# Writing the engine loops over pairs of experts out as straight code with constant waits, in a two-layer decoder with eight routed experts

## The reference, cut to what matters

```
logits = (t @ w_router).astype(jnp.float32)
top_v, top_i = lax.top_k(logits, TOP_K)                 # TOP_K = 2
top_w = jax.nn.softmax(top_v, axis=-1)
combine = jnp.sum(jax.nn.one_hot(top_i, N_EXPERTS) * top_w[..., None], axis=1)
out = jnp.zeros_like(t)
for e in range(N_EXPERTS):                              # N_EXPERTS = 8
    out = out + combine[:, e:e+1] * swiglu(t, w1[e], w3[e], w2[e])
# swiglu(x, w1, w3, w2) = (silu(x @ w1) * (x @ w3)) @ w2
# w1, w3: 1024 x 2816, w2: 2816 x 1024, float32
```

## Time and profile before

| what | value |
|---|---|
| median of 3 executions | 1356.41 us (1354.2 to 1357.6) |
| the profiled execution | 1354.73 us, of which the span of its instructions 1350.5 us |
| instructions in the profile | 17653 |
| PE busy | 1312.4 us, 97% |
| DVE busy | 1061.7 us, 79% |
| ACT busy | 877.3 us, 65% |
| POOL busy | 65.6 us, 5% |
| HBM read | 376.12 MB, 282 GB/s over the span |

### The profile page before, as it was taken

How to read it: one execution, slowest core, us unless ns; L and a number is a source line. 1 busy time by engine, 2 the same in 40 slices (tenths; PEclk the granted TensorE clock), 3 DMA queues, 4 the chain that set the end, 5 groups by cost and what they waited for, 6 DMA issues and landing times.

```text
span 1350.5 us, 17653 instructions
## 1 busy us (share of the span) xinstructions
PE 1312.4 (97%) x6066; PEld 1076.6 (80%) x6066; DVE 1061.7 (79%) x983; ACT 877.3 (65%) x870; POOL 65.6 (5%) x45
## 2 busy tenths in 40 slices
PE   7899999999999999799999999999999999999998
PEld 6688888888888788678888778788888788788776
DVE  5857756665457667699898799898898897998996
ACT  6567444444365664577777677777777777777774
POOL 0500000000006010000000000000000000000200
PEclk9999999999999999899999999999999999999999
DMA  9654546555555544289998899998999997999993
GB/s 360 242 190 133 167 146 221 184 187 187 192 183 175 168 150 163 94 302 369 388 384 324 316 410 372 377 374 293 389 405 380 368 357 281 411 386 385 410 355 141
DMA packets 105488, 382.12 MB, mean 283 GB/s; under 512 B 11952, under 2 KB 11952, under 8 KB 105392
## 3 DMA queue, kind: packets, MB, share of 16 engines
q1 hardware_dynamic: 103632, 375.11, 76.2%
q0 software_dynamic: 1616, 5.77, 1.1%
q10 hardware_dynamic: 144, 0.01, 0.0%
HBM read 376.12 MB, written 4.72 MB: 282 GB/s over the span
## 4 chain that ended last, share of the span: by engine, by line
PE 83%; DVE 6%; DMA 5%; ACT 2%; issue 2%; POOL 1%; SPq 1%; POOLq 0%; DVEq 0%; ACTq 0%
PE ps L391 26%; PE ps L393 25%; PE ps L392 25%; DMA raw<-in_units 4%; DVE wl L386 3%; PE ps L881 3%; ACT wh L378 1%; PE ps L1175 1%; DMA cols<-y_rows,yidx 1%; DMA y_rows<-xs 1%; POOL rst L514 1%; PE ps L933 0%; SPq L371 0%; DVE turn_t L1350 0%; POOL back L562 0%
## 5 line engine op out<-in xcount | busy, mean ns | idle before, releaser
L386 DVE TENSOR_TENSOR wl<-raw,wh 128x2048 fp32r<-128x2048 f32 x351 | 802.3, 2295 | 179.2 <-ACT wh L378 170.8
L378 ACT ACTIVATE wh<-raw 128x2048 fp32r<-128x2048 f32 x351 | 673.7, 1920 | 227.0 <-PE ps L393 206.3
L391 PE MATMUL ps<-wh,XT_h 128*128 128x512 f32 x1228 | 491.3, 400 | 15.4 <-DVE wl L386 12.7
L393 PE MATMUL ps<-wh,XT_l 128*128 128x512 f32 x1228 | 480.4, 391 | 0.0
L392 PE MATMUL ps<-wl,XT_h 128*128 128x512 f32 x1228 | 479.3, 390 | 0.0
L391 PEld LDWEIGHTS ps<-wh,XT_h 128*128 128x128 f32 x1228 | 231.1, 188 | 68.0 <-DVE wl L386 12.5
L393 PEld LDWEIGHTS ps<-wh,XT_l 128*128 128x128 f32 x1228 | 231.0, 188 | 50.3
L392 PEld LDWEIGHTS ps<-wl,XT_h 128*128 128x128 f32 x1228 | 231.5, 189 | 44.9
L391 PE MATMUL ps<-wh,moe_gT_h 128*128 128x512 f32 x352 | 138.0, 392 | 0.0
L393 PE MATMUL ps<-wh,moe_gT_l 128*128 128x512 f32 x352 | 137.1, 390 | 0.0
L392 PE MATMUL ps<-wl,moe_gT_h 128*128 128x512 f32 x352 | 137.0, 389 | 0.0
(11 more groups left out here) (235 smaller groups left out, 909.9 us busy)
## 6 DMA issues: line engine op xcount, KB each, us to landing
raw<-in_units SPq DMA_DIRECT2D x704, 512.0 KB, 5.9
y_rows<-xs POOLq DMA_DIRECT2D x7, 512.0 KB, 7.4
mix<-in_xT SPq DMA_DIRECT2D x2, 512.0 KB, 5.6
raw<-in_units SPq DMA_DIRECT2D x4, 256.0 KB, 8.4
h<-in_x SPq DMA_DIRECT2D x1, 1024.0 KB, 12.1
out<-h SPq DMA_DIRECT2D x2, 512.0 KB, 3.0
rows<-in_rows SPq DMA_DIRECT2D x1, 896.0 KB, 15.1
cols<-in_cols SPq DMA_DIRECT2D x1, 512.0 KB, 14.5
```

What stands on the lines that cost most here:

```text
L378: nc.scalar.activation(wh[:, U.split_slot(j), :], raw[:, U.raw_slot(j), :], ACT.Copy).then_inc(hi_ready, 1)
L386: nc.vector.tensor_tensor(wl[:, s, :], raw[:, U.raw_slot(j), :], wh[:, s, :].bitcast(F32), ALU.subtract).then_inc(lo_ready, 1)
L391: nc.tensor.matmul(o, xh, bh, start=start, stop=False)
L393: return nc.tensor.matmul(o, xl, bh, start=False, stop=stop)
```

## The change

The loops over pairs of SP, POOL, ACT, PE and DVE are written out: Python loops over the experts issue the same calls with integers in place of the loop's register. All waits get constants, and SP's DRAM addresses become constants. The calls for each expert, their order, the places and the data are those of before. The loop over overflows is not touched.

```
--- before.py
+++ after.py
@@ -478,12 +478,9 @@
                     U = Units(DENSE_BASE)
                     for u in range(FFN_UNITS):
                         load_unit(sp, U, u, DENSE_BASE + u)
-            with sp.Fori(0, E // 2) as i:
-                U = Units(MOE_BASE, i, 2 * FFN_UNITS)
-                for half in range(2):
-                    for u in range(FFN_UNITS):
-                        j = half * FFN_UNITS + u
-                        load_unit(sp, U, j, 2 * FFN_UNITS * i + (MOE_BASE + j))
+            U = Units(MOE_BASE)
+            for j in range(E * FFN_UNITS):
+                load_unit(sp, U, j, MOE_BASE + j)
 
             sp.wait_ge(table_ready, 1)
             n_over = sp.value_load(otab[0:1, 0:1], min_val=0, max_val=3)
@@ -551,10 +548,8 @@
                 rows_of = y_d[0:Y_ZERO, :].rearrange("(e r) d -> e r d", r=P)[p]
                 pool.dma_start(rows_of, xs3[:, b, :]).then_inc(y_sent, 16)
 
-            store_rows(0, 0)
-            with pool.Fori(0, E // 2 - 1) as i:
-                store_rows(2 * i + 1, 1)
-                store_rows(2 * i + 2, 0)
+            for p in range(E - 1):
+                store_rows(p, p % 2)
             pool.wait_ge(yidx_ready, 1)
             pool.wait_ge(y_sent, 16 * E)
             for t in range(TT):
@@ -860,12 +855,10 @@
 
             gather_copy(0, 0)
             gather_copy(0, 1)
-            expert(0, 0, Units(MOE_BASE), 0, FFN_UNITS + 1, None)
-            with act.Fori(0, E // 2 - 1) as i:
-                U = Units(MOE_BASE + FFN_UNITS, i, 2 * FFN_UNITS)
-                expert(2 * i + 1, 1, U, 0, FFN_UNITS + 1, 8 * i + 8)
-                expert(2 * i + 2, 0, U, FFN_UNITS, FFN_UNITS + 1, None)
-            expert(E - 1, 1, Units(MOE_BASE), (E - 1) * FFN_UNITS, FFN_UNITS - 1, None, None, 0)
+            U = Units(MOE_BASE)
+            for p in range(E - 1):
+                expert(p, p % 2, U, p * FFN_UNITS, FFN_UNITS + 1, 4 * p + 4 if p % 2 else None)
+            expert(E - 1, 1, U, (E - 1) * FFN_UNITS, FFN_UNITS - 1, None, None, 0)
             act.wait_ge(table_ready, 1)
             n_over = act.value_load(otab[0:1, 0:1], min_val=0, max_val=3)
             with act.If(n_over > 0):
@@ -1241,12 +1234,10 @@
             for t in range(TT):
                 last = nc.tensor.matmul(ps[:, 3, 0:E], ones[:, :], routed[:, t, :], start=t == 0, stop=t == TT - 1)
             last.then_inc(counted, 1)
-            expert(0, 0, Units(MOE_BASE), 0, None, 8, None)
-            with pe.Fori(0, E // 2 - 1) as i:
-                U = Units(MOE_BASE + FFN_UNITS, i, 2 * FFN_UNITS)
-                expert(2 * i + 1, 1, U, 0, None, 8 * i + 8, (2 * i + 4, 8 * i + 8))
-                expert(2 * i + 2, 0, U, FFN_UNITS, None, 8 * i + 16, None)
-            expert(E - 1, 1, Units(MOE_BASE), (E - 1) * FFN_UNITS, None, 4 * E, None, 0)
+            U = Units(MOE_BASE)
+            for p in range(E - 1):
+                expert(p, p % 2, U, p * FFN_UNITS, None, 8 * ((p + 2) // 2), (p + 3, 4 * p + 4) if p % 2 else None)
+            expert(E - 1, 1, U, (E - 1) * FFN_UNITS, None, 4 * E, None, 0)
             pe.wait_ge(table_ready, 1)
             n_over = pe.value_load(otab[0:1, 0:1], min_val=0, max_val=3)
             with pe.If(n_over > 0):
@@ -1762,12 +1753,9 @@
                     for r in range(4):
                         add_back(scatter_at, e, r)
 
-            expert(0, 0, Units(MOE_BASE), 0, 0, rank, FFN_UNITS + 1, None)
-            with dve.Fori(0, E // 2 - 1) as i:
-                U = Units(MOE_BASE + FFN_UNITS, i, 2 * FFN_UNITS)
-                expert(2 * i + 1, 1, U, 0, 2 * i + 1, rank, FFN_UNITS + 1, 2 * i + 2)
-                expert(2 * i + 2, 0, U, FFN_UNITS, 2 * i + 2, rank, FFN_UNITS + 1, None)
             U = Units(MOE_BASE)
+            for p in range(E - 1):
+                expert(p, p % 2, U, p * FFN_UNITS, p, rank, FFN_UNITS + 1, p + 1 if p % 2 else None)
             expert(E - 1, 1, U, (E - 1) * FFN_UNITS, E - 1, rank, FFN_UNITS - 1, None, 0)
             dve.wait_ge(table_ready, 1)
             n_over = dve.value_load(otab[0:1, 0:1], min_val=0, max_val=3)
```

## The result

| | before | changed |
|---|---|---|
| median of 5 executions | 1354.2 us (1351.49 to 1357.6) | 1343.73 us (1342.63 to 1346.29) |
| profiled execution | 1354.73 us | 1346.29 us |
| its span | 1350.5 us | 1344.2 us |
| outside the span | 4.23 us | 2.09 us |

The ratio is 0.9926, interval 0.9902 to 0.9949: 10 us less, where 7.6 were forecast (1356.41 - 1348.8, from the median of three on record).

The account below looks back on a forecast made before the run. PE, busy 97% of the span, was taken as the bound; 3.54 us from PE's branches and 3.56 from SP's, off 1356.41, gave 1349.3, taken as 1348.8 us. The 8-in-10 range was 1345.5 to 1353.5.

Parts of the forecast that it names:

- The reading of the bound: Whole kernel: PE is busy for 97% of the span, so only what makes PE stand still can be won.
- step 1: Where experts 3 and 5 begin: PE's two branches back go, giving 1.45 + 2.09 = 3.54 us.
- Step 2: At the start of experts 2, 4 and 6: SP's three branches back go, giving 3.56 us.
- only the branches of PE count: Rival, experts 2 and 6: late units come from DMA traffic after each gather, SP's silence only coincides; 1352.9 us, chance 0.18.
- Step 3: Engines' waits: constants in place of computed ones change nothing, cost 0, as register instructions are hidden or fall into idle time.
- its span and what lies around it: Whole execution of 1354.73 us: taken as span 1350.5 us and 4.23 us around it.
- step 4: Added code: nothing runs that did not run, instruction reads stay the same, and the final part just comes earlier.
- The base: Whole kernel: the starting time was 1356.41 us, the median of the runs shown, 1.7 us above the profiled execution.
- The guess that the spread would shrink: Between runs: part of the spread may be SP's silences of varying length, which would go.
- memory sets the pace: Rival, even experts: once PE stops pausing, weights come late and the time is given back; 1356 us, chance 0.10.
- straight code is read too late: Rival, PE's written-out code: sequential reads miss, about 1.77 us at each of 23 blocks; about 1390 us, chance 0.06.

Follow-up runs that it names:

- before_pad: Kernel before plus 205 never-executed instructions in PE's overflow loop, moving PE's last code to 179 in its block: 1355.07 us against 1355.04, ratio 0.999.
- pe_only: Kernel before with only PE's loop written out: 1347.06 us, ratio 0.9949.
- sp_pe: Kernel before with the loops of SP and PE written out, those of ACT, DVE and POOL kept: 1345.18 us, ratio 0.993.
- rest_only: Kernel before with only the loops of ACT, DVE and POOL written out: 1355.6 us against 1354.3, ratio 1.0002.
- after_pad: Changed kernel plus 51 never-executed instructions in PE's overflow loop, moving PE's last code to 230 in its block: 1346.57 us, ratio 0.9934.
- after2: Changed kernel, unchanged, run again for a second profile: 1344.56 us.
- before: The kernel before the change, with its loops: median 1354.2 us, profiled execution 1354.73 us.
- both: Changed kernel with DVE's last-expert row additions moved behind its last split and PE's last wait moved into the untaken overflow branch: 1339.12 us, ratio 0.9874.
- after_pad2: Changed kernel with the same 51 never-executed instructions, run again beside the unpadded changed kernel on one chip: 1347.37 us.
- after: First profile of the changed kernel: profiled execution 1346.29 us, median 1343.73 us, ratio 0.9926.
- before2: Kernel before, unchanged, run again for a second profile: 1354.47 us.
- pause: Changed kernel with added PE waits, without a branch, where experts 1, 3, 5 and 7 begin: 1356.41 us, ratio to the kernel before 1.0019.

## Why the prediction was wrong, point by point

- **The reading of the bound and step 1's mechanism: right, its size too small.** Both gaps were the branch, and nothing took their place. 3.54 us is what that one profile held; other profiles of looped PE code show 4.0 to 5.2 us, and up to 1.7 us (2.8 in before_pad) of slow clock behind a gap. No row of the profile read had a clock under 1.00 in the experts, so the prediction had no such term. By the median spans, `pe_only` gained 1350.2 - 1344.65 = 5.55 us, 2 more than forecast.
- **Step 2: right in kind, too large in size.** With PE straight, SP's silences cost 1.7 us in the profile and 1.9 in the median, not 3.56; in the profile read they had cost more in expert 2. That the sum fits (7.10 forecast for the experts, 7.30 between the two profiles, 5.55 + 1.85 = 7.4 by the median spans) is luck: one term was too small by about as much as the other was too large. The rival "only the branches of PE count" is refuted by sp_pe against pe_only. It counted expert 4, which lost nothing at its start, against the silence; that silence was the shortest of the three (5.53 us, against 7.71 and 6.39). SP's rounds end 18.3 us before PE gets there (762.53 - 744.20), not 17; no term uses it.
- **Step 3: right.** No cost is seen in rest_only, and the even experts of sp_pe stand at the floor of 92.77 us with these loops in place.
- **The step that failed is "its span and what lies around it", with step 4.** The 4.23 us around the span were carried over as a constant, and the final branch was to "just come earlier". They became 2.09 us, since the longer code moves the end of PE's code within its block; after_pad, with 51 instructions more, gives the time back. By the medians of all executions measured with after2 it went from 3.95 to 2.14, by 1.8 us. This is a side effect of the layout and not of the missing branches, and by after_pad 51 instructions more would have lost it.
- **The base, also wrong.** The forecast of 1348.8 stood on a median of 3 runs, 1356.41. With 5 runs it was 1354.2, and in four further sets of 12 to 23 executions 1354.21 to 1355.04. Against 1354.2 the same forecast of 7.10 us gives 1347.1; the 2.1 us outside the span bring it to 1345.0. The 1.7 us put on top of the profiled execution for the median were not there. Had either the base or the outside been right, the time would have lain within the range: the low end would be 1345.5 - 2.2 = 1343.3 us by the base, or 1345.5 - 2.1 = 1343.4 by the outside, and 1343.73 was measured. The remaining 1.3 us are within the spread: the profiled execution of the changed kernel is its slowest of five, and the start of the experts differs between its two profiles by 1.3 us. The guess that the spread would shrink came true: the 23 executions of before in one set span 6.6 us, the six of sp_pe 1.2.
- **The rivals "memory sets the pace" and "straight code is read too late": both refuted.** The even experts run at 376 to 379 GB/s with PE busy all the time, SP waits longer for free places than before, and no gap shows inside an expert. The Trainium skill's limit of about 358 GB/s ("DMA: Bandwidth & Descriptors", "Where 436 GB/s comes from") did not bind here; its rule that a taken branch forces a fetch ("Runtime: NRT & Kernel Launch", "Instruction fetch mechanics") agrees with the trace, which has one 16 KB packet within each branch back on PE and 4.6 to 6.4 us for the branch.

SP's waits in the changed kernel, over its experts:

```profile
SPq L371 <- DVE wl L386: 543.9, 256, 24.2
```

## What to carry to other kernels

Look for loops at the places where equal work takes unequal time, and price a branch back on the bounding engine by its row: here 4.6 to 6.4 us, of which the engine's queued work hides 3.1 to 3.25. Remove it first there; a branch on a feeding engine counted here only for 0.3 to 2.6 us of its 5.5 to 7.7, and once for nothing. Sum over the whole time and not the span alone, for what lies around the span is not a constant when the code's length changes, and take a base from more than three runs if the effect is under 1%.

## What the runs showed that was not expected

- The place of PE's last code within 256 instructions is worth about 2 us: outside the span lie 2.1 to 2.5 us in every execution with the end at or near 179 (the changed kernel, both, before_pad and others), 3.5 to 4.5 us in every one with it at or near 230. No other place was measured.
- TensorE's clock fell to 1.2 GHz behind pauses of 2.54, 2.68, 2.76, 2.82, 2.92 and 3.38 us, and not behind others of 2.62, 2.88 and 2.92 us, nor behind any of nine between 1.68 and 2.31 us where odd experts begin. In expert 7 it fell behind pauses of 2.13, 2.15, 2.17 and 2.29 us (after_pad2, after_pad, sp_pe, after), and not behind one of 2.22 us in after2, nor behind shorter ones there (1.53 to 2.02 us). Ahead of each of these pauses PE had run for 75 us or more without one over 0.7 us. So with much the same work before it, the length of a pause alone does not decide, and one under 2.5 us is not safe.
- SP's branch back silences it for 7.71 us in a stage where weight DMAs are dense, and costs 0.3 to 0.9 us each time in pe_only (6.20 to 6.85 us of silence) and up to 2.6 us in the first profile. That the six places of `raw` cover the rest fits this and was not tested.
- The wait of PE near 59 us, in the front part that the change does not touch, leaves 3.4 to 5.2 us between two starts of PE. PE waits there for a split of DVE, and ahead of it small DVE steps take some seven times their length while POOL works beside them. In the changed kernel a pair of 128x32 steps took 2.57 us, and one took 0.18 us once POOL's steps of 1.3 us each were nearly over:

```profile
55.95 2.57 DVE L1341 TENSOR_TENSOR turn_t<-sin,rows 128x32 f32<-128x32 f32 x2
58.44 1.42 DVE L1341 TENSOR_TENSOR turn_t<-cos,rows 128x32 f32<-128x32 f32 x2
...
61.07 0.18 DVE L1341 TENSOR_TENSOR turn_t<-cos,rows 128x32 f32<-128x32 f32 x1
```

In sp_pe the same pair took 1.38 us, and PE's wait was 1.1 us shorter:

```profile
55.63 1.38 DVE L1345 TENSOR_TENSOR turn_t<-sin,rows 128x32 f32<-128x32 f32 x2
```

That the two engines hinder each other was read from these rows and not tested. It is not what makes the executions differ: from the first of these steps to the end of the split behind them it is 8.7 us in after and in after2, and 8.5 in sp_pe. Between after and after2, expert 0 begins 1.34 us apart; 0.59 of it is there when PE goes on behind the wait (63.63 and 63.04 us), and the rest comes behind it. There the clock stood at 1.2 GHz for 6.8 us in the profiles with 5.08 to 5.17 us between the starts (after, before, before2, before_pad, rest_only), for 3.4 us in the ten with 3.75 to 4.97 us, and not at all in pause, with 3.40 us:

```profile
63.63 0.80 PE L391 MATMUL ps<-wh,XT_h 128*128 128x512 f32 x1 [4.72 <-DVE wl L386]
64.22 0.63 PE L392 MATMUL ps<-wl,XT_h 128*128 128x512 f32 x1
```

```profile
62.42 0.50 PE L391 MATMUL ps<-wh,XT_h 128*128 128x512 f32 x1 [3.01 <-DVE wl L386]
62.76 0.40 PE L392 MATMUL ps<-wl,XT_h 128*128 128x512 f32 x1
```

The first is after, the second pause. Expert 0 began at 571.29 us in after and at 567.86 in pause, and this is a part of the spread of all medians here.
